# A two-part change to a hybrid decoder trunk: where the adaLN projection runs, and in which order the GLA tiles' steps are issued

## The reference

```
mods = (silu(c) @ w_ada[l] + b_ada[l]).reshape(B, 9, D)      # sh1 sc1 g1 sh2 sc2 g2 sh3 sc3 g3
y = swiglu(x * (1 + sc1) + sh1)            ; x = LN(ALPHA*x + (1 + g1) * 0.5 * y)
y = mixer (x * (1 + sc2) + sh2)            ; x = LN(ALPHA*x + (1 + g2) * y)
y = swiglu(x * (1 + sc3) + sh3)            ; x = LN(ALPHA*x + (1 + g3) * 0.5 * y)

def gla_mixer(h, s0):
    q, k, v, g_lr, r = split(h @ w_in)
    la = log_sigmoid(g_lr @ w_gate2 + b_gate) / 16
    o, s = recurrence over chunks of q, k, v, la from state s0
    o = o * rsqrt(mean(o*o) + eps) * g_onorm
    return (o * silu(r)) @ w_out
```

## Time and profile before

| What | Value |
|---|---|
| runs before, median of 3 | 5123.63 us (4994.98 to 5393.65) |
| the profiled execution: time, span | 4996.93 us, 4995.4 us |
| spans of the 8 cores in it | 4976.2 to 4995.4 us |
| PE busy | 3744.6 us (75%) |
| DVE, ACT, POOL busy | 1519.9, 1690.9, 169.0 us |
| DMA moved | 329.09 MB, mean 66 GB/s |
| mean granted TensorE clock, core 6 | 0.815 |

### The profile page before, as it was taken

One profiled execution on the slowest core, in us unless ns is written; L12 is line 12 of the kernel. 1 busy time (PEld: TensorE's weight loads), 2 busy tenths in 40 slices (PEclk: granted clock), 3 DMA queues, 4 the chain that ended last, 5 costly groups with the idle time before them and its releaser, 6 DMA issues.

```text
span 4995.4 us, 62404 instructions; the slowest of 8 cores (4976.2 to 4995.4 us)
## 1 busy us (share of the span) xinstructions
PE 3744.6 (75%) x21114; PEld 1702.8 (34%) x21426; DVE 1519.9 (30%) x2504; ACT 1690.9 (34%) x3180; POOL 169.0 (3%) x306
## 2 busy tenths in 40 slices
PE   0698957566569896468989578888888855679894
PEld 0343423222224343233444223333333333434442
DVE  0113133333321323232131333333433343331313
ACT  0123133444432312322221345444454433332312
POOL 0000000000000000000000000000000000000000
PEclk9999988787769998789999766666766555689997
DMA  9643441221234344884433301111001024133332
GB/s 196 115 72 58 71 80 34 51 51 31 52 80 72 62 72 81 149 191 87 69 62 67 71 7 24 24 24 24 9 16 24 22 77 119 52 51 69 63 66 91
DMA packets 147058, 329.09 MB, mean 66 GB/s; under 512 B 61824, under 2 KB 90880, under 8 KB 142400
## 3 DMA queue, kind: packets, MB, share of 16 engines
q0 software_dynamic: 66784, 226.73, 26.9%
q1 hardware_dynamic: 79968, 98.36, 6.6%
HBM read 515.26 MB, written 36.50 MB: 110 GB/s over the span
## 4 chain that ended last, share of the span: by engine, by line
PE 67%; ACT 9%; DVE 8%; issue 7%; DMA 7%; another core or an unknown queue 1%; DVEq 0%; ACTq 0%; SPq 0%; POOL 0%; POOLq 0%
PE psF L554 23%; PE psF L575 12%; PE psF L968 5%; PE psF L996 5%; DMA arenaB<-w_ada 4%; ACT arenaB L395 3%; DVE arenaF L493 2%; PE psF L993 2%; PE psF L1044 2%; PE psF L1010 2%; PE psF L1007 1%; PE psF L755 1%; DVE arenaF L494 1%; DMA arenaF<-cache_k_d 1%; PE psF L1107 1%
## 5 line engine op out<-in xcount | busy, mean ns | idle before, releaser
L554 PE MATMUL psF<-arenaB 128*128 128x512 bf16 (+1 forms) x6897 | 1281.4, 341 | 95.9 <-ACT arenaF L556 45.7
L554 PEld LDWEIGHTS psF<-arenaB 128*128 128x128 bf16 x7040 | 595.0, 98 | 781.6 <-issue 138.1
L575 PE MATMUL psF<-arenaB 128*128 128x512 bf16 (+1 forms) x3484 | 645.2, 337 | 2.1 <-issue 0.2
L558 DVE TENSOR_TENSOR arenaB<-psF,arenaF 128x512 bf16<-128x512 f32 (+1 forms) x440 | 253.7, 587 | 981.1 <-PE psF L554 878.7
L556 ACT ACTIVATE arenaF<-psF 128x512 f32<-128x512 f32 (+1 forms) x440 | 224.3, 511 | 874.0 <-PE psF L554 873.9
L575 PEld LDWEIGHTS psF<-arenaB 128*128 128x128 bf16 x3520 | 293.6, 97 | 334.2 <-issue 2.9
L968 PE MATMUL psF<-arenaB 128*128 128x512 bf16 (+1 forms) x923 | 307.8, 453 | 132.3 <-ACT arenaB L395 88.0
L997 ACT ACTIVATE arenaB<-psF 128x256 bf16<-128x256 f32 (+1 forms) x768 | 257.8, 336 | 307.5 <-PE psF L996 298.5
L449 ACT ACTIVATE arenaB<-x 128x512 bf16<-128x512 f32 (+1 forms) x240 | 130.6, 544 | 677.1 <-DVE x L414 453.3
L414 DVE SCALAR_TENSOR_TENSOR x<-psF,mods,x 128x512 f32<-128x512 f32 x192 | 143.8, 751 | 676.8 <-PE psF L575 401.9
L395 ACT ACTIVATE arenaB<-x,mods 128x512 bf16<-128x512 f32 x416 | 297.5, 800 | 106.3 <-PE psF L376 106.0
(11 more groups left out here) (152 smaller groups left out, 3566.8 us busy)
## 6 DMA issues: line engine op xcount, KB each, us to landing
arenaB<-w_up POOLq DMA_DIRECT2D x176, 512.0 KB, 5.2
arenaB<-w_dn POOLq DMA_DIRECT2D x64, 704.0 KB, 7.3
arenaB<-w_ada POOLq DMA_DIRECT2D x8, 2304.0 KB, 24.5
arenaB<-w_ada POOLq DMA_DIRECT2D x24, 768.0 KB, 13.3
arenaB<-w_in_v POOLq DMA_DIRECT2D x5, 2048.0 KB, 14.5
arenaB<-w_in_r POOLq DMA_DIRECT2D x5, 2048.0 KB, 14.1
arenaB<-w_outa POOLq DMA_DIRECT2D x5, 2048.0 KB, 14.4
arenaB<-vscr SPq DMA_DIRECT2D x16, 520.0 KB, 6.5
```

What stands on the lines that cost most here:

```text
L554: P.add("pe", lambda e, o=o, lt=lt, rh=rh, k=k: e.matmul(o, lhsT=lt, rhs=rh, start=(k == 0), stop=(k == KC - 1)), reads=[lt, rh], writes=[o])
L558: P.add("dve", lambda e, go=go, sa_=sa_, pu=pu: e.tensor_tensor(out=go, in0=pu, in1=sa_, op=ALU.mult), reads=[pu, sa_], writes=[go])
L575: P.add("pe", lambda e, Y=Y, lt=lt, rh=rh, kk=kk: e.matmul(Y, lhsT=lt, rhs=rh, start=(kk == 0), stop=(kk == NJ - 1)), reads=[lt, rh], writ ...
```

## The change

First, `ada_gen` takes a range of pieces and a list of the entries to derive. Ahead of the first FFN it does pieces 0 to 2 alone (shift, scale and gate of the first FFN). Pieces 3 to 7 become a generator `bg` inside `ffn(0, 0)`, in chunks of 384 columns (15 chunks, two buffers, PSUM bank 6), stepped once after each tile step of the up-projection. Second, the body of the GLA tile loop is cut into four functions, and these are issued in another order; the modulate of the next tile moves to the end of `st_vr`.

```diff
-    def ada_gen(l, bufs, noc, bank):
+    def ada_gen(l, bufs, noc, bank, pcs=range(8), entries=DERIVE_ALL):
         nb_ = 0
-        for pc in range(8):
+        for pc in pcs:
...
-    for _ in ada_gen(0, wada_buf, 9, 0):
+    for _ in ada_gen(0, wada_buf, 9, 0, pcs=range(0, 3), entries=DERIVE_ALL[0:1] + DERIVE_ALL[3:4]):
         pass
...
+        bg = None
+        if ada_bg:
+            bg = ada_gen(0, [arenaB.take([128, KC, 384]) for _ in range(2)], 3, 6, pcs=range(3, 8),
+                         entries=DERIVE_ALL[1:3] + DERIVE_ALL[4:6])
...
                     if pend_ln is not None:
                         next(pend_ln, None)
+                    if bg is not None:
+                        next(bg, None)
...
-        for ti, (lo, n) in enumerate(all_tiles):
+        def st_laqk(ti):
+            lo, n = all_tiles[ti]
             smp = lo >= T
-            modulate(ht, lo, [(lo, n)], mod_t, sh_oc, sc_oc)
+            if ti == 0:
+                modulate(ht, lo, [(lo, n)], mod_t, sh_oc, sc_oc)
...
+        def st_vr(ti):
...
                 so = sR[:, c, 0:n]
                 P.add("act", lambda e, so=so, rp=rp: e.activation(out=so, in_=rp, func=AF.Silu), reads=[rp], writes=[so])
+            if ti + 1 < len(all_tiles):
+                nlo, nn = all_tiles[ti + 1]
+                modulate(ht, nlo, [(nlo, nn)], mod_t, sh_oc, sc_oc)
+
+        def st_rec(ti):
...
+        def st_out(ti):
...
+        st_laqk(0)
+        st_vr(0)
+        for ti in range(nT):
+            st_rec(ti)
+            if ti + 1 < nT:
+                st_laqk(ti + 1)
+            st_out(ti)
+            if ti + 1 < nT:
+                st_vr(ti + 1)
...
-    stages = [lambda: ffn(0, 0), gla_phase, ...
+    stages = [lambda: ffn(0, 0, ada_bg=True), gla_phase, ...
```

More of the change, by code:

```diff
@@ L323, in build_program, with derive @@
     P.add("act", lambda e: e.activation(out=sct, in_=cin_sb, func=AF.Silu), reads=[cin_sb], writes=[sct])
-    def derive(mt):
-        for i, coef in ((1, None), (4, None), (7, None), (2, 0.5 / ALPHA), (5, 1.0 / ALPHA), (8, 0.5 / ALPHA)):
+    DERIVE_ALL = ((1, None), (4, None), (7, None), (2, 0.5 / ALPHA), (5, 1.0 / ALPHA), (8, 0.5 / ALPHA))
+    def derive(mt, entries=DERIVE_ALL):
+        for i, coef in entries:
             v = mt[:, i * 8:(i + 1) * 8, :]
@@ L351, in ada_gen @@
                 yield 1
-        pv = mk(psF[:, bank, 0:360], [psF[:, bank, 0:360].ap[0], (5, 72), (1, 5)])
-        bb = bcast_last(bada_sb[:, l, :], 5)
-        mo = mods[:, l]
+        o0, o1 = min(pcs) * 9, (max(pcs) + 1) * 9
+        pv = mk(psF[:, bank, o0 * 5:o1 * 5], [psF[:, bank, o0 * 5:o1 * 5].ap[0], (5, o1 - o0), (1, 5)])
+        bb = bcast_last(bada_sb[:, l, o0:o1], 5)
+        mo = mods[:, l, o0:o1, :]
         P.add("dve", lambda e, mo=mo, pv=pv, bb=bb: e.tensor_tensor(out=mo, in0=pv, in1=bb, op=ALU.add),
-              reads=[pv, bada_sb[:, l, :]], writes=[mo])
-        derive(mo)
+              reads=[pv, bada_sb[:, l, o0:o1]], writes=[mo])
+        derive(mods[:, l], entries)
         yield 0
@@ L514, in ln_bufs, with ffn @@
         return d
-    def ffn(l, which):
+    def ffn(l, which, ada_bg=False):
         fi = l * 2 + which
@@ L584, in ffn @@
             pend_ln = ln_finish(st, li, defer=(hi == 0))
+        if bg is not None:
+            for _ in bg:
+                pass
     def gla_phase():
@@ L706, in gla_phase @@
         all_tiles = [(0, 512), (512, 512), (1024, 512), (1536, 512), (2048, 16)]
[L707 removed]
+        def st_laqk(ti):
+            lo, n = all_tiles[ti]
             smp = lo >= T
[L709 removed]
+            nch = 4
+            ctok = 4 if smp else 128
+            if ti == 0:
+                modulate(ht, lo, [(lo, n)], mod_t, sh_oc, sc_oc)
             gp = psF[0:16, 6, 0:n]
@@ L744, in gla_phase @@
                 P.add("dve", lambda e, ko=ko, kp=kp, tk=tk: e.tensor_tensor(out=ko, in0=kp, in1=tk, op=ALU.mult), reads=[kp, tk], writes=[ko])
+        def st_vr(ti):
+            lo, n = all_tiles[ti]
+            smp = lo >= T
+            nch = 4
+            ctok = 4 if smp else 128
             wv_ = load_w(w_in_v)
@@ L792, in gla_phase @@
             ln_finish(st, li)
+        nT = len(all_tiles)
+        st_laqk(0)
[7 more added lines that the diff above has]
+                st_vr(ti + 1)
     KS_OFF, QS_OFF = 52700, 52830
@@ L1205, in build_program @@
     lnF = None
-    stages = [lambda: ffn(0, 0), gla_phase, lambda: ffn(0, 1), kv_phase, lambda: ffn(1, 0), attn_phase, lambda: ffn(1, 1)]
+    stages = [lambda: ffn(0, 0, ada_bg=True), gla_phase, lambda: ffn(0, 1), kv_phase, lambda: ffn(1, 0), attn_phase, lambda: ffn(1, 1)]
     for si, fn_ in enumerate(stages):
```

## The result

The changed kernel is faster by half a percent, less than forecast: the ratio to the kernel before is 0.9945 (95% interval 0.9932 to 0.9959), about 27.5 us of 5000. The median of ten runs is 4974.88 us (4966.6 to 5334.71), that of ten runs of before 5064.12 (4994.98 to 5393.65). In some executions the cores of one die or of both show a lower granted clock than the others and take longer, so the ratios in this text are taken over the remaining ones alone. The profiled execution has a span of 4968.7 us, 26.7 less than before's 4995.4. Its chain that ended last has kept its shape, against the earlier trace rows: TensorE 66%, DMA 8% instead of 7%.

A forecast was written before the change was run, and what follows sets the result against it. The prediction took TensorE's own work, two thirds of the span, as the bound, with DMA full before the first FFN. It summed 4996.9 - 22.7 (first part) - 11.3 (GLA) = 4963 us, range 4930 to 5020.

The forecast's parts named there:

- the landing of w_adakv 0: Ahead of the first FFN: issued at 80.6, 2.05 us start-up and 12.5 us transfer, landing at 95.1.
- the price of a chunk: DMA time per w_ada chunk under the first FFN: 4.9 us, between bounds of 4.58 and 7.76.
- GLA: Gain from reordering the GLA tiles: 11 us in all, range 3 to 20.
- the turns between tiles: GLA, transposes to next recurrence: 94.4 us instead of 101.8, 7.4 less in each of three prompt-tile turns, 22 in all.
- Start of the first FFN: First FFN starts at 112.1 instead of 178.75, 66.6 us earlier.
- The burst of chunks: First up-projection: 15 chunks and seven w_up at DMA's pace from 112.1, the last chunk landing at 207.6.
- The slower rival: First FFN: a chunk costs 7.76 us as in the K/V stage; 5006 us with the GLA gain, 5017 without; chance 0.12.
- pause in v: GLA turn: TensorE stands some 15 us before v's second chunk, whose bank copy waits on ACT behind pass 2.
- the three recurrences: First three GLA recurrences: modulate ahead of ACT's first copy delays the state update 5.7 us each, 17 in all.
- the turn into the sample tile: GLA, transposes' end to v's second chunk: 48.3 us instead of 54.4, gain 6.
- The table load: GLA: one more ACT table load of 1.28 us per turn, rather than the skill's 2.66 with drain.
- Full cover: Rival: chunks run under the FFN without stall, LayerNorm and modulate cost TensorE nothing; 4856 us, chance 0.04.

The follow-up runs named there:

- the four edits together: Changed kernel with a chunk every third tile step, pass 2 behind v copies, modulate inside the recurrence, prologue buffers swapped; ratio 0.9699 to the kernel before.
- the last kernel: Kernel of the four edits together, with both w_adakv pieces also moved under the first FFN as six chunks; ratio 0.9672 to the kernel before.

## Why the prediction was right and where it was off

The mechanisms held, each confirmed by an edit that takes it away. Two things failed: the step from the profile to the runs, and the size of three terms of the sum.

The forecast took 34 us off before's profiled execution, a ratio of 0.993; the two profiles differ by 26.7 (44.8 against before's second profile), the ratio gives 27.5. The figure of 4963 stands 12 below the measured median of 4974.88, inside the range. But beside the median shown for before, 5124, it reads as a gain of 160 us, which no term of the sum held. That median was of three runs, 4995, 5124 and 5394; with ten it was 5064, and half of those ten lie at 4995 to 5005. I wrote that my time was on the profiled execution's scale and then did not turn it into a ratio. That 4963 lies so near 4975 says little: a second profile of the unchanged kernel came out 18 us above the first.

The mis-sized terms are the landing of w_adakv 0, the price of a chunk, and in GLA the turns between tiles. The gain up to the end of the up-projection was 17.3 us instead of 22.7, a quarter less; GLA's was a tenth less, and there the terms were further off than their sum.

- **Start of the first FFN**: forecast 112.1, measured 115.64 on the slowest core. Piece 2 landed 1.1 us later than I had it. The mis-sized term is the transfer behind it: w_adakv 0 took 99.89 - 81.71 = 18.2 us from issue to landing, not 2.05 + 12.5. Its start-up was 2.3 us, near my 2.05 (issue at 81.71, first bytes behind 84); the rest took 15.9 us at 144 GB/s, where I had reckoned with the full pace of the pieces before. On the early core of each pair it took 14.4 to 15.3 us, as in my sum, and those four cores started at 110.0 to 110.7. So the term held on half of the cores and failed on the half that holds the slowest one; why they differ stays open. That nothing was in flight beside piece 2 was right, and the swap of buffers gave back 4 to 7 us, my 5.
- **The burst of chunks**: forecast 95.5 us from the first FFN matmul to the last chunk, measured 98.6. I took 4.9 us per chunk, it was 5.1: nearer to the low bound of 4.58 than to the 7.76 of the K/V stage, as argued, since nothing is written out here. The 29 tile steps behind it took 1.1 us less than I had. Together that makes the 17.3 us at the end of the up-projection (332.3 to 314.98). The slower rival, decided at 6.4 us per chunk, was never near.
- **TensorE goes cold in the pauses** (5.3 us for 16 matmuls). DMA sets the pace of the burst all the same: the run with every second step, where the pauses are short, gives nearly the same price per chunk, 5.2. How much of the 3 us above my 95.5 is clock and how much transfer was not separated.
- **GLA**: forecast 11.3, measured 10.4 between the slowest cores, 10.2 between the medians. The steps of the first turn came out as drawn: turn 94.4 forecast, 95.5 measured; output projection 19.5 and 19.8; pause in v some 15 forecast, 15.6; cold start behind it 1.5 forecast, 1.4 to 2.8 measured (5.06 to 6.37 against 3.61). But part of the agreement of the sum is luck. The three turns gained 20.3 us, not 22; the three recurrences lost 15.2, 5.1 each and not 5.7; the turn into the sample tile gained 3.6, not 6. The errors nearly cancel, and the last 1.9 us were won behind that turn, where I had no term.
- **The table load**: one more in each of the four turns, 1.28 us between DVE's subtraction and ACT's Sqrt (885.97 to 887.26). The Trainium skill (ScalarE: Activation LUTs, "What ACT_TABLE_LOAD costs") adds a drain of about 1.4 us to a switch. No switch in the changed kernel's timeline shows it: the Sqrt follows 0.01 us behind the load on an ACT that had been idle, and on a busy ACT it is no different. At 1422.03 a load follows an activation within 0.02 us, and the next activation comes at 1423.33, 0.02 us behind the load. The measured 1.3 us stands, as the sum had it.
- **Full cover**, the rival of 4856 us: the four edits together come to it (4859 in the profile). In the change it failed for the reasons given against it: the chunks are asked for in the first third of the half, and the v copy stands behind pass 2.
- **Behind GLA** I had assumed the same time to the microsecond. The spread there is 11 us between executions, as large as the whole GLA term, and a forecast made against one profile carries it.

## What to carry to other kernels

Background transfers need a rate, not only a place: the whole half had DMA time for the fifteen chunks (146 of 164 us), but asked for twice per column they exceeded it and cost 46 of the 64 us won; every third step costs 10, the small matmuls' own time. And when tiles are software-pipelined on in-order queues, follow the engine that copies PSUM out: TensorE's next work may be free and ready, but it stops at the second use of its bank if that copy is queued behind the previous tile's normalisation. Moving LayerNorm's eight pass-2 blocks behind the four copies was worth more than five times the pipelining itself (56 us against 10).

## What the runs showed of the hardware that was not expected

In the profiled execution of the last kernel two of the eight cores, 2 and 3, took 590.3 and 589.4 us for the third FFN and all others 562.9 to 564.3. Windows of the same stretch on core 1 and core 2 (columns as in the earlier trace rows) show TensorE busy almost without a break on both, but a granted clock of 0.81 on core 2. Core 1:

```profile
2470.00:2530.00 60.00, 60.00 (x393) 28.97 (x391) 12.54 (x25) 11.02 (x24) 4.23 (x8) 1.00 0.46 84
```

Core 2:

```profile
2410.00:2470.00 60.00, 58.07 (x318) 25.55 (x315) 10.83 (x22) 10.24 (x22) 3.72 (x7) 0.81 0.39 61
2470.00:2530.00 60.00, 60.00 (x331) 26.53 (x330) 9.86 (x21) 9.65 (x21) 4.78 (x9) 0.81 0.37 57
```

Core 3 shows the same 0.81, core 0 stays at 1.00 like core 1. The pair was back at 1.00 by 2590 us. What lowered it is not known; it is 26 us on one stage, as much as the whole change is worth, and it decided which core was the slowest.
